# The conditioning product of a two-block network: from TensorE to VectorE multiply-adds, with its weight slabs given other places in the stream

## What is computed

```python
cs = jax.nn.silu(c)                        # (1, 1024)
mod = cs @ w_ada[l] + b_ada[l]             # w_ada: (1024, 6144)
sh_a, sc_a, gt_a, sh_f, sc_f, gt_f = jnp.split(mod, 6, axis=-1)
h = modulate(rms_norm(x, g_mix[l]), sh_a, sc_a)
u = h @ w_in[l]                            # (256, 9728): retention q, k, v, gate; attention q, k, v; gates
ret = retention(...); att = dilated_attention(...)
merged = sigmoid(ga) * (ret @ w_ret_o[l]) + sigmoid(gb) * (att @ w_att_o[l])
x = x + gt_a * (merged @ w_o[l])
h = modulate(rms_norm(x, g_ffn[l]), sh_f, sc_f)
x = x + gt_f * moe(h, ...)                 # 4 of 32 experts for each token
```

## Time and profile before

| | before |
|---|---|
| median of 3 runs | 2115.82 us (2113.66 to 2119.99) |
| span of the profiled execution | 2114.5 us |
| PE busy in it | 1962.1 us, 93% |
| DVE busy | 688.3 us, 33% |
| ACT busy | 636.7 us, 30% |
| moved by DMA | 592.99 MB |

### The profile page before, as it was taken

One profiled execution on the slowest core, in us unless ns is written; L12 is line 12 of the kernel. 1 busy time (PEld: TensorE's weight loads), 2 busy tenths in 40 slices (PEclk: granted clock), 3 DMA queues, 4 the chain that ended last, 5 costly groups with the idle time before them and its releaser, 6 DMA issues. The chain is left out here.

```text
span 2114.5 us, 27736 instructions
## 1 busy us (share of the span) xinstructions
PE 1962.1 (93%) x11194; PEld 1255.6 (59%) x11195; DVE 688.3 (33%) x1010; ACT 636.7 (30%) x893; POOL 11.3 (1%) x23
## 2 busy tenths in 40 slices
PE   5999998799999999999999999997979998988998
PEld 1888776553443344344434434445869986878997
DVE  2545443520111111011101101113664555645555
ACT  2433455211111111111111111113544443644442
POOL 0000000000000000000000000000000000000000
PEclk6999998979999999999999999998989998989999
DMA  9467753199999999999999999975634554434552
GB/s 357 151 206 266 268 165 109 27 367 400 413 407 408 408 413 410 402 414 411 407 407 411 408 406 412 411 297 185 208 122 161 181 188 133 161 111 145 180 170 109
DMA packets 193239, 592.99 MB, mean 280 GB/s; under 512 B 10572, under 2 KB 85472, under 8 KB 157297
## 3 DMA queue, kind: packets, MB, share of 16 engines
q1 hardware_dynamic: 190944, 583.95, 72.6%
q0 software_dynamic: 2224, 8.04, 1.1%
HBM read 590.88 MB, written 1.07 MB: 280 GB/s over the span
## 5 line engine op out<-in xcount | busy, mean ns | idle before, releaser
L1256 PE MATMUL psum<-expert_ring,expert_arena 128*64 128x512 f32 x2048 | 449.3, 597 | 0.0
L1256 PEld LDWEIGHTS psum<-expert_ring,expert_arena 128*64 128x64 f32 x2048 | 144.8, 138 | 302.8 <-issue 302.8
L313 DVE TENSOR_TENSOR layer_w_lo<-layer_ring,layer_w_hi 128x1024 fp32r<-128x1024 f32 x190 | 231.3, 1224 | 247.7 <-ACT layer_w_hi L308 247.5
L308 ACT CAST layer_w_hi<-layer_ring 128x1024 fp32r<-128x1024 f32 x190 | 197.8, 1047 | 248.2 <-PE psum L358 122.9
L356 PE MATMUL psum<-layer_x_hi,layer_w_hi 128*128 128x256 f32 x864 | 248.6, 288 | 13.4 <-DVE layer_w_lo L313 10.3
L357 PE MATMUL psum<-layer_x_lo,layer_w_hi 128*128 128x256 f32 x864 | 247.5, 286 | 0.0
L358 PE MATMUL psum<-layer_x_hi,layer_w_lo 128*128 128x256 f32 x864 | 247.3, 286 | 0.0
L1276 PE MATMUL psum<-expert_ring,expert_arena 128*64 128x512 f32 x1024 | 226.8, 595 | 0.0
L1179 DVE TENSOR_SCALAR expert_arena<-psum 128x512 f32<-128x512 f32 x32 | 22.1, 692 | 537.5 <-PE psum L1256 537.5
L356 PEld LDWEIGHTS psum<-layer_x_hi,layer_w_hi 128*128 128x128 f32 x864 | 169.1, 196 | 16.0 <-issue 12.0
L1094 ACT COPY expert_arena<-psum 128x256 f32<-128x256 f32 x32 | 11.9, 372 | 541.9 <-PE psum L1260 541.9
(11 more groups left out here) (262 smaller groups left out, 2155.4 us busy)
## 6 DMA issues: line engine op xcount, KB each, us to landing
expert_ring<-in_w_mlp_dram SPq DMA_DIRECT2D x384, 1024.0 KB, 8.6
layer_ring<-in_w_ffn_in_dram SPq DMA_DIRECT2D x44, 1024.0 KB, 5.1
mixer_ring<-in_w_in_dram SPq DMA_DIRECT2D x38, 1024.0 KB, 7.3
mixer_ring<-in_w_ada_dram SPq DMA_DIRECT2D x24, 1024.0 KB, 6.3
layer_ring<-in_w_ffn_out_dram SPq DMA_DIRECT2D x20, 1024.0 KB, 5.1
layer_ring<-in_b_w_in_dram SPq DMA_DIRECT2D x10, 1024.0 KB, 9.7
layer_ring<-in_w_mix_out_dram SPq DMA_DIRECT2D x8, 1024.0 KB, 5.1
layer_ring<-in_a_w_in_dram SPq DMA_DIRECT2D x7, 1024.0 KB, 9.6
```

Of the source, the lines that this page charges most:

```text
L308: self.nc.scalar.copy(hi, raw).then_inc(self.hi_ready, 1)
L313: self.nc.vector.tensor_tensor(lo, raw, hi.bitcast(FP32), ALU.subtract).then_inc(self.lo_ready, 1)
L1256: last = nc.tensor.matmul(U[CAP * h:CAP * h + CAP, N * n:N * n + N], xg[:, k, :], ring[:, at:at + N], start=False, stop=k == UP - 1)
```

## The change

Each slot of `w_ada` is now 256 rows by 1024 columns (two chunks of 128 rows, four slots for one group of 1024 columns, six groups). VectorE multiplies each chunk, row by row, by the conditioning number of that row, and adds it to a running sum of 128 by 1024 (`take`). When a group's four slots are in, one matmul with ones adds up the 128 partitions, and a second adds the bias. For groups 0 and 1 this is done in the jobs `mod0` to `mod3` themselves, into all 128 partitions. For groups 2 to 5 it is done in jobs `ada2` to `ada5`, into 32 partitions each, and the copy and the spreading of rows stay. A slot of `w_ada` is now released by VectorE, when its second multiply-add is done. The sixteen later slots start after `aq5`: `aq5`, `ak0` to `ak5`, `av0`, `av1`, and the rounds 0 to 6 of attention have one each.

```diff
     def piece(self, name, slots):
         job = Job(name, None, list(slots), [])
         self.list.append(job)
-        self.parts += 1
-        self.raw_released[slots[-1]] = ("part", self.parts)
+        self.taken += 1
+        job.freed = self.taken
+        self.raw_released[slots[-1]] = ("taken", self.taken)
...
+    ada_sums = [free(arena, 8192, D), free(arena, 9216, D)] + [free(base, 3072, D)] * 4
+    mod4 = const(M, "decay", 2, N)
...
-    def ada_slot(g, k):
-        return jobs.raw(A["w_ada"][0, k * P:(k + 1) * P, SLOT * g:SLOT * (g + 1)].rearrange("p (k n) -> p k n", k=4))
-    ada_left = [(g, k) for g in (1, 2) for k in range(KC)]
+    def ada_piece(g, j):
+        jobs.piece(f"ada{g}.{j}", jobs.raw(A["w_ada"][0, 2 * P * j:2 * P * (j + 1), D * g:D * (g + 1)].rearrange("(k p) n -> p k n", p=P)))
+    ada_left = [(g, j) for g in range(2, 6) for j in range(4)]
+    ada_whole = []
     def some_ada():
+        if ada_whole:
+            jobs.add(f"ada{ada_whole.pop()}", "dve", bank=BANKS - 1)
         if ada_left:
-            g, k = ada_left.pop(0)
-            if k < KC - 1:
-                jobs.piece(f"ada{g}.{k}", ada_slot(g, k))
-            else:
-                jobs.add(f"ada{g}", "dve", ada_slot(g, k), bank=BANKS - 1)
+            g, j = ada_left.pop(0)
+            ada_piece(g, j)
+            if j == 3:
+                ada_whole.append(g)
...
-    for k in range(KC - 1):
-        jobs.piece(f"ada0.{k}", ada_slot(0, k))
-    jobs.add("ada0", "dve", ada_slot(0, KC - 1), bank=BANKS - 1)
+    for g in range(2):
+        for j in range(4):
+            ada_piece(g, j)
...
-            some_ada()
+            if what == "ak" or n == 5:
+                some_ada()
...
+            def take(job):
+                g, j = int(job.name[3]), int(job.name[5])
+                at = (job.slots[0] % RING_MIX) * SLOT
+                stream.wait_here(dve, job.slots[0])
+                for k in range(2):
+                    rows, c = ring[:, at + D * k:at + D * k + D], cs[:, 2 * j + k:2 * j + k + 1]
+                    if j + k == 0:
+                        step(nc.vector.tensor_scalar(ada_sums[g], rows, c, None, ALU.mult))
+                        continue
+                    if k == 0:
+                        dve.wait_ge(stream.taken, job.freed - 1)
+                    ins = nc.vector.scalar_tensor_tensor(ada_sums[g], rows, c, ada_sums[g], ALU.mult, ALU.add)
+                    if k == 0:
+                        step(ins)
+                    else:
+                        ins.then_inc(stream.taken, 1)
...
                 elif name.startswith("ada"):
                     g = int(name[3:])
-                    ada_products(b, job.slots[0], KC - 1)
-                    for j in range(4):
-                        pick = ident[0:12, 4 * g + j:4 * g + j + 1].to_broadcast([12, 32])
-                        last = nc.tensor.matmul(b[32 * j:32 * j + 32, :], pick, b12[:, :], start=False, stop=True)
+                    pe.wait_ge(stream.taken, 4 * (g + 1))
+                    for n in range(2):
+                        r = 32 * (2 * (g % 2) + n)
+                        nc.tensor.matmul(b[r:r + 32, :], ones[:, 0:32], ada_sums[g][:, N * n:N * n + N], start=True, stop=False)
+                        last = bias_of(b[r:r + 32, :], 2 * g + n, 32)
                 elif name.startswith("mod"):
                     n = int(name[3:])
-                    wait_freed(pe, f"ada{n // 4}")
-                    r = 32 * (n % 4)
-                    last = nc.tensor.matmul(b, ones[r:r + 1, :], mod4[r:r + 1, n // 8, :], start=True, stop=True)
+                    if n < 4:
+                        pe.wait_ge(stream.taken, 4 * (n // 2 + 1))
+                        nc.tensor.matmul(b, ones, ada_sums[n // 2][:, N * (n % 2):N * (n % 2) + N], start=True, stop=False)
+                        last = bias_of(b, n, P)
+                    else:
+                        wait_freed(pe, f"ada{n // 2}")
+                        r = 32 * (n % 4)
+                        last = nc.tensor.matmul(b, ones[r:r + 1, :], mod4[r:r + 1, n // 8, :], start=True, stop=True)
```

More of the change, by code:

```diff
@@ L146, in __init__ @@
         self.list, self.by_name, self.counts, self.last_in = [], {}, {"act": 0, "dve": 0}, {}
-        self.jobs = self.highs = self.parts = 0
+        self.jobs = self.highs = self.parts = self.taken = 0
         self.slots, self.units, self.released, self.raw_released = [], [], {}, {}
@@ L261, in __init__ @@
         self.nc, self.jobs, self.ring, self.ring_slots, self.high, self.low = nc, jobs, ring, ring_slots, high, low
-        self.full, self.part = sem("full"), sem("part_done")
+        self.full, self.part, self.taken = sem("full"), sem("part_done"), sem("slot_taken")
         self.freed = {"act": sem("freed_by_act"), "dve": sem("freed_by_dve")}
@@ L268, in wait_tensor @@
         which, n = release
-        eng.wait_ge(self.full if which == "full" else self.part, n)
+        eng.wait_ge({"full": self.full, "part": self.part, "taken": self.taken}[which], n)
     def wait_freed(self, eng, name):
@@ L438, in mixer @@
     negmax, mx2, lsum, rsum = small[:, 80:82], free(small, 84, 2, 2), free(small, 88, 2, 2), small[:, 92:94]
-    csb = free(small, 128, KC, 32)
     c8, b12 = arena[0:KC, 4096:4096 + P], M["b12"]
@@ L519, in mixer @@
         some_ada()
-    assert not filler and not ada_left
+    assert not filler and not ada_left and not ada_whole
     for half in range(2):
@@ L705, in _ @@
                 if job.index is None:
+                    take(job)
                     continue
@@ L737, in _ @@
                     dve.wait_ge(full, job.index + 1)
-                    nc.vector.tensor_copy(mod4[:, int(name[3:]) // 2, :], b).then_inc(freed_by_dve, 1)
+                    g = int(name[3:])
+                    r = slice(2 * 32 * (g % 2), 2 * 32 * (g % 2) + 2 * 32)
+                    if g == 2:
+                        wait_freed(dve, "rs7")
+                    nc.vector.tensor_copy(mod4[r, g // 2 - 1, :], b[r, :]).then_inc(freed_by_dve, 1)
                     continue
@@ L833, in _, with bias_of @@
             pe.wait_ge(tiny_here, 32)
-            def ada_products(b, q, k):
-                stream.wait_here(pe, q)
-                at = (q % RING_MIX) * SLOT
-                for j in range(4):
-                    last = nc.tensor.matmul(b[32 * j:32 * j + 32, :], csb[:, k, :], ring[:, at + N * j:at + N * j + N], start=k == 0, stop=False)
-                return last
+            def bias_of(b, n, width):
+                pick = ident[0:12, n:n + 1].to_broadcast([12, width])
+                return nc.tensor.matmul(b, pick, b12[:, :], start=False, stop=True)
             for job in jobs.list:
@@ L845, in _ @@
                 if job.index is None:
[L846 to L851, removed]
                     continue
```

5 lines of the change are left out of this document (1 added, 4 removed).

## The result

The changed kernel takes 2169.14 us (median of 4 runs, 2168.16 to 2169.4), the one before 2117.87 us (4 runs): a ratio of 1.0244, with a 95% interval of 1.0227 to 1.026. Predicted were 2159 us, with 2137 to 2172.

A forecast was written before the change was run, and what follows sets the result against it. TensorE's instructions bound the kernel before; a closed ring of waits would bound the wide jobs after. 44.3 - 3.0 + 1.0 + 1.4 = 43.7 us gave a span of 2158.2, with the median 2159 us, range 2137 to 2172.

The forecast's parts named there:

- The closed ring: From aq5 to av2: each take's release gates loads, casts and splits that precede the next take; av2 44.3 us late.
- W(n+2): Wide slot of the job two after job n; its load queues behind the next job's w_ada slot, awaiting a release.
- A turn: Wide jobs, release to release: 8.0 landing and cast, 3.4 splits, 1.2 copy, 2.6 take; 15.2 us against 7.0 needed.
- The signs that the prediction named: From 165 to 270 us TensorE idles some 45 us in five or six gaps; from 300 us work shifts about 42.
- The time for a load: Two loads in a turn: the trace's 8.0 us was used; the skill's rule gave 6.8 and a total of 2153.
- The jobs ada2 to ada5: TensorE's jobs of 8 instructions for the later groups: taken at 2.0 us each, some of them in gaps.
- the lower clock in `av1`: In av1, after TensorE's idling: 2.0 us added, between nothing and 11.
- The start: First w_ada slots: takes done at 37.6, scale first used at 44.52, 6.9 us for two jobs; costed at nothing.
- The rounds of attention: After av2: three groups gone from TensorE -3.0, ada4 +1.0, round 6's exposed take +1.4, ada5 in gaps.
- The faster one: Wide jobs: wide loads not held by the w_ada release, turns of 7.0 us, total 2107; chance 0.06.
- The clock: Rival: TensorE at half clock through ak2 to av2, some 60 us, total 2176 or more; chance 0.05.
- The third rival: Wide jobs: only three or four turns close late, turns of 9 to 10 us, total 2110 to 2122; chance 0.03.

The follow-up runs named there:

- e1: Changed kernel with w_ada and wide slots numbered and loaded in VectorE's order of use: 2120.42 us against 2116.17 before, ratio 1.0021.
- e2: Changed kernel, old order of loads, with the sixteen later w_ada slots starting in the first wide job: 2208.34 us, ratio 1.0428.
- e5: Changed kernel with the edits of e1 and e2 together: 2116.72 us against 2116.57 before, ratio 0.9997.
- e3: Changed kernel with later w_ada slots loading 64 of 1024 columns: 3140.29 us, unusable as routing changed; experts begin at 488.4 us against 501.6.
- e6: e1 with bias matmuls ahead of the wait at the start, and both ones before both biases in ada jobs: 2111.7 us, ratio 0.9976.
- e7: Changed kernel with all edits of e5 and e6: 2105.63 us against 2116.57 before, ratio 0.9943.
- e9: e5 with bias matmuls ahead of the wait at the start: 2115.25 us against 2116.65 before, ratio 0.9987.
- e4: Changed kernel with multiply-adds of later w_ada slots 8 columns wide instead of 1024, first products whole: 2148.64 us, ratio 1.0162.
- e8: Kernel before, unchanged, profiled again: second block's layer 642.4 us against 637.7 in the first profile; experts begin at 450.0 instead of 452.4.

## Why the prediction was right, step by step

The number came out 10 us low, near the top of the range (2169 for 2159, up to 2172). The mechanism that the prediction names is the one that the runs show; what was off are the sizes of terms beside it.

**The closed ring is shown.** e1 changes only the order of loads and takes all but 4 of the 51 us away; e2 puts more turns into it and adds 39; e5 puts as many turns into the opened ring and adds none. The prediction's reason also says why the order matters: with W(n+2) behind A(n+1) in the queue, the take that stands after the splits of W(n+2) on VectorE is what lets W of the next job load. In VectorE's order of use no load stands behind one that waits for a later take.

**A turn** was put at 15.2 us, measured 15.4 and 15.3, and the one with the normalisation at 20.7, measured 20.95. Its parts too: release to cast 8.0 (measured 8.1 to 8.4; once 9.6), a take 2.6 (measured 2.60). The first release came at 169.97 (predicted 169.2), the fifth at 235.96 (234.5), the one that lets `av1`'s slots load at 262.68 (259.9). `av1` started at 273.0 for 271. Of these 2.8 us, 1.6 are the one wait of 9.6 us: the first slot of `av0` landed that much later than the others, and nothing shows why. The signs that the prediction named are there, with other sizes: from 165 to 270 us TensorE idles 36 us in five gaps of 4 to 15 us (some 45 were named), and from attention on the work is shifted by 47 to 49 us, not 42.

**The time for a load.** The one of the Trainium skill, "DMA: Bandwidth & Descriptors", section "Anatomy of one DMA", gave 2153. That section gives the time for transfers that GpSimd issues, while SyncE issues these; the prediction carried it over without saying so. The runs side with the row: 8.1 us for the pair. e3 adds that a pair with hardly any bytes in its first half still takes 6.1.

**The jobs ada2 to ada5 were mis-sized.** The prediction took 2.0 us each. In series at full clock they took 3.9. At half clock, which it had left out for them, `ada2` took 7.4 (221.67 to 229.04 in the kernel after); that one lay in a wait there, so that of the error only `ada3` showed: `av2` started at 291.71 for 287.5, 48.5 late for 44.3, 2.0 of it the late `av1` and 1.9 the job. The 2.0 us for the lower clock in `av1` was nearly right: it cost about 2.3.

**The start was costed at nothing, and took 2.3.** The first projection's matmuls begin at 56.80 instead of 54.47. The step that failed is that "two jobs have to run after 37.6, and they have 6.9 us": no time was put against the 6.9. The jobs took 8.1, and began 1.7 us later. TensorE in the kernel after:

```profile
39.31 2.08 PE L881 MATMUL psum<-mixer_arena,common_consts 128*128 128x512 f32 x2 [5.45 <-DVE mixer_arena L701]
41.32 2.07 PE L851 MATMUL psum<-b,common_consts 12*128 12x512 f32 x2
43.32 2.08 PE L881 MATMUL psum<-mixer_arena,common_consts 128*128 128x512 f32 x2
45.33 2.07 PE L851 MATMUL psum<-b,common_consts 12*128 12x512 f32 x2
```

The takes ended at 39.3 (predicted 37.6), and the two jobs last until 47.4, 2.0 us for each pair; VectorE's scale waits 1.32 for the last. Half clock may be a part of it: a pair of `ada2` took 1.85 us at a granted clock of 0.50 and one of `ada3` 0.97 at 1.00. But here the granted clock reads 1.00 while the pairs take 2.0, so the rows don't settle it. With the bias ahead of the wait (e6, e7) the first projection starts at 55.23 and 55.49: 1.3 to 1.6 of the 2.3 come back at the start. That they reach the total isn't shown (e9).

**The rounds of attention.** `ada4` cost nothing (1.0 predicted), it lay in the gap whole. Round 6 and `ada5` cost 3.7 together (1.4 predicted), if the three groups that left TensorE gave the 3.0 of the sum: the experts begin at 501.6 instead of 452.4, 49.2 late, where the prediction had 43.7. With light multiply-adds and an `ada5` of the same length 4.6 us of the rounds go (e4), so the 3.7 hang on the takes there, more than on `ada5` alone. The span grew by 51.8; the other 2.6 us lie behind the beginning of the experts, where the code is the same: the second block's layer took 641.0 us for 637.7, and e8 shows such differences between executions of one kernel. So that part of the miss is chance. Each slot taken out of TensorE ahead of `aq5` gave 1.2 us, not 1.0.

**The rivals.** The faster one, 2107, named the condition on which it turns, a W that is not held by the release of A(n-1). e1 made just that, and e7 with the other costs mended reached 2105.6. The clock stayed at half only in pieces (0.76 in the stretch, 1.00 after it). The third rival, effects that cancel, needed turns of 9 to 10 us; they took 14.3 and more.

## What to carry to other kernels

When the engine that releases a shared buffer changes, lay out, for one turn, what must happen before the release, which loads stand behind the waiting one on their queue, and whether one of these loads feeds the releasing engine ahead of its next release. If so, the sum of that chain is the period once it is longer than the work of each engine in a turn, however idle everybody is; issue the loads in the order in which the releasing engine uses them, and the same work may be free. Once a wait ahead of a few small matmuls is gone, look at their order too: neighbours of one kind that write different quarters of the columns overlapped, the same matmuls in another order took up to twice as long.

## What the runs showed of the hardware

- A 32-column matmul of 128x512 fp32 is two instructions, and the pair took 0.97 us at full clock and 1.85 at half. Four such pairs on two quarters took 3.9 us in the order ones, bias, ones, bias; 2.9 as ones, bias of the other quarter, bias, ones; and 2.0 as ones, ones, bias, bias.
- Of two 1 MB loads issued 0.4 us apart, the second was ready 8.1 us after the first issue; with the first one cut to a sixteenth, 6.1 (e3). The first of two such loads was ready 5.0 us after its issue. Ready is told by the cast that waited for it.
- The multiply-add took 1.28 us for 128x1024 with the slot in the ring as a source, as in the earlier trace rows, and 0.24 for 128x8.
- In nine of twelve profiles some of the first 14 matmuls of the first projection follow each other every 0.43 us, for up to 2.9 us of loss; in the other three all follow every 0.23. The kernel before did both: at a granted clock of 0.50 from 55 to 57 us in its first profile, and of 1.00 in e8. In the kernel after the granted clock reads 1.00 throughout the start although its first six matmuls are slow, so that there the reading doesn't follow the durations.
